# Neighbourhood attention in a two-layer hybrid block: one attention step takes a query block of one head, or of both heads of a pair side by side on the array's rows

## What is computed

```python
s_loc = jnp.einsum('bwhd,bwkhd->bhwk', qr, kw).astype(jnp.float32) + bias
s_ctx = jnp.einsum('bwhd,bshd->bhws', qr, k_ctx).astype(jnp.float32)
p = jax.nn.softmax(jnp.concatenate([s_loc, s_ctx], axis=-1), axis=-1).astype(v.dtype)
return (jnp.einsum('bhwk,bwkhd->bwhd', p[..., :n_keys], vw)
        + jnp.einsum('bhws,bshd->bwhd', p[..., n_keys:], v_ctx))
```

## Time and profile before

| | |
|---|---|
| Median of 3 runs (lowest, highest) | 2354.46 us (2350.59, 2357.75) |
| Profiled execution: its time, its span | 2355.82 us, 2354.0 us |
| TensorE busy | 2267.7 us, 96% of the span |
| VectorE, ScalarE busy | 1283.7 us (55%), 841.1 us (36%) |
| TensorE's granted clock, mean | 0.987 |
| Attention stage, layer 0 | 458.90 to 592.97 us, 134.07 us |
| Attention stage, layer 1 | 1604.68 to 1738.74 us and its last 1.5 us |

### The profile page before, as it was taken

One profiled execution on the slowest core, in us unless ns is written; L12 is line 12 of the kernel. 1 busy time (PEld: TensorE's weight loads), 2 busy tenths in 40 slices (PEclk: granted clock), 3 DMA queues, 4 the chain that ended last, 5 costly groups with the idle time before them and its releaser, 6 DMA issues.

```text
span 2354.0 us, 33977 instructions
## 1 busy us (share of the span) xinstructions
PE 2267.7 (96%) x14512; PEld 2131.6 (91%) x14512; DVE 1283.7 (55%) x1979; ACT 841.1 (36%) x1327; POOL 86.8 (4%) x160
## 2 busy tenths in 40 slices
PE   7999988999989999999979999999999999999997
PEld 3999988999978999999969999999999799999996
DVE  3555577466746867667475555225655533343434
ACT  4555332355335221221265444224543431222212
POOL 0000010000000000000000000000000000000000
PEclk9999999999999999999999999999999999999999
DMA  6212155221533543433412121232223222222121
GB/s 244 86 64 69 62 176 164 100 73 62 180 90 137 173 137 128 150 117 126 108 44 86 63 63 60 81 96 82 71 93 126 72 90 81 72 69 84 54 90 45
DMA packets 59750, 233.62 MB, mean 99 GB/s; under 512 B 7312, under 2 KB 7344, under 8 KB 57424
## 3 DMA queue, kind: packets, MB, share of 16 engines
q1 hardware_dynamic: 41040, 153.12, 20.0%
q0 software_dynamic: 18560, 78.33, 9.7%
HBM read 223.00 MB, written 8.42 MB: 98 GB/s over the span
## 4 chain that ended last, share of the span: by engine, by line
PE 86%; DVE 6%; ACT 3%; issue 2%; DMA 2%; DVEq 0%; ACTq 0%; SPq 0%; POOL 0%; POOLq 0%
PE unit L402 16%; PE unit L403 16%; PE unit L405 16%; PE unit L390 11%; PE unit L392 10%; PE unit L391 10%; DVE junk L1372 2%; PE sc L390 1%; DMA raw<-w_main 1%; PE unit L483 1%; PE sc L392 1%; PE sc L391 1%; DVE wl L1272 1%; DVE ptl L1282 1%; PE tp L654 1%
## 5 line engine op out<-in xcount | busy, mean ns | idle before, releaser
L402 PE MATMUL unit<-hmh,wh 128*128 128x320 f32 x2304 | 694.1, 309 | 1.2 <-issue 0.8
L403 PE MATMUL unit<-hml,wh 128*128 128x320 f32 x2304 | 694.0, 309 | 0.0
L1272 DVE TENSOR_TENSOR wl<-raw,wh 128x1024 fp32r<-128x1024 f32 x276 | 335.4, 1223 | 360.4 <-ACT wh L937 353.8
L405 PE MATMUL unit<-hmh,wl 128*128 128x320 f32 x2304 | 525.0, 309 | 0.0
L402 PEld LDWEIGHTS unit<-hmh,wh 128*128 128x128 f32 x2304 | 432.5, 188 | 3.3 <-issue 1.9
L403 PEld LDWEIGHTS unit<-hml,wh 128*128 128x128 f32 x2304 | 432.6, 188 | 1.5
L405 PEld LDWEIGHTS unit<-hmh,wl 128*128 128x128 f32 x2304 | 385.2, 188 | 0.0
L937 ACT ACTIVATE wh<-raw 128x1024 fp32r<-128x1024 f32 x276 | 283.8, 1049 | 120.4 <-DMA raw<-w_main 120.4
L1372 DVE CUSTOM_DVE_ANT_0 junk<-ada,csb,par 128x1024 f32<-128x1024 f32 x160 | 205.6, 1285 | 23.7 <-DMA ada<-w_ada 4.0
L390 PE MATMUL unit<-wh,hmh 128*128 128x256 f32 (+1 forms) x640 | 201.1, 314 | 12.1 <-DVE hml L1282 5.1
L392 PE MATMUL unit<-wh,hml 128*128 128x256 f32 (+1 forms) x640 | 199.3, 311 | 0.0
(11 more groups left out here) (282 smaller groups left out, 3476.0 us busy)
## 6 DMA issues: line engine op xcount, KB each, us to landing
raw<-w_main SPq DMA_DIRECT2D x276, 512.0 KB, 3.7
ada<-w_ada POOLq DMA_DIRECT2D x80, 512.0 KB, 3.9
bias<-biases POOLq DMA_DIRECT2D x16, 640.0 KB, 5.0
first<-w_first SPq DMA_DIRECT2D x8, 1024.0 KB, 21.0
x<-x POOLq DMA_DIRECT2D x2, 2560.0 KB, 12.1
gains<-g_rows POOLq DMA_DIRECT2D x4, 1024.0 KB, 5.2
x_keep<-x POOLq DMA_DIRECT2D x1, 2560.0 KB, 10.2
x<-x_keep POOLq DMA_DIRECT2D x1, 2560.0 KB, 9.6
```

The costliest lines, as they stand in the source:

```text
L402: pe.matmul(u[:, h, 0:n], a[0], xs[h][0], start=f, stop=False)
L403: pe.matmul(u[:, h, 0:n], a[0], xs[h][1], start=False, stop=False)
L405: mm = pe.matmul(u[:, h, 0:n], a[1], xs[h][0], start=False, stop=z)
L1272: dve.tensor_tensor(wl[slot[i]][:, :], raw[slot[i]][:, :], f32(wh[slot[i]][:, :]), ALU.subtract)\
```

## The change

A step is now one query block of both heads of a pair, so `STEPS` is 20 per layer. `score` issues the matmuls of the two heads in turn: head 0 on the array's rows 0 to 63 into one bank, head 1 on rows 64 to 127 into the other. `turn` transposes both heads, and the pieces come behind both, not half ahead of them. `weigh` takes each head's group one after the other, and each head has a PSUM bank of its own. The transposed weights `pth` and `ptl` of head 1 are new buffers, and they lie in slots 2 and 3 of the slabs. So slabs 46 to 55 (`NARROW` to `WIDE`) go into slots 0 and 1 alone, and `WIDE` is 56. The biases are loaded and negated in three parts. The halves of the sums are added in two parts. The splits are at steps 3, 6, 8, 11, 13, 16 and 20.

```diff
-WIDE, W_O, LAST = 58, 64, 130
+NARROW, WIDE, W_O, LAST = 46, 56, 64, 130
...
-STEPS = NPAIR * 10
+STEPS = NPAIR * 5
...
-        pth = n1("pth", [P, 2, 2, NS], F32R); ptl = n1("ptl", [P, 2, 2, NS], F32R)
+        pth = [n1("pth", [P, 2, 2, NS], F32R), at("pth1", [P, 2, 2, NS], wl_at + (RING + 2) * SLAB * 4, F32R)]
+        ptl = [n1("ptl", [P, 2, 2, NS], F32R), at("ptl1", [P, 2, 2, NS], wl_at + 2 * SLAB * 4, F32R)]
...
-            return min(32, -(-(v + 1) * 33 // 10)) if p < NPAIR - 1 else min(32, -(-(v + 1) * 8 // 3))
+            return min(32, -(-(j + 1) * 33 // 5)) if p < NPAIR - 1 else min(32, -(-(j + 1) * 32 // 7))
...
-        LIN_AT = [[3, 5, 7, 10]] * (NPAIR - 1) + [[3, 6, 9, 12]]
+        LIN_AT = [[1, 2, 3, 4]] * (NPAIR - 1) + [[1, 3, 5, 6]]
...
+        SPLIT_AT = (3, 6, 8, 11, 13, 16, 20)
...
-            may = range(RING) if j < WIDE or LAST <= j < LAST + 4 else range(RING, RING + MORE) if j >= LAST - 2 else range(RING + MORE)
+            may = range(2) if NARROW <= j < WIDE else range(RING) if j < WIDE or LAST <= j < LAST + 4 else range(RING, RING + MORE) if j >= LAST - 2 else range(RING + MORE)
...
-                    if g >= 2:
-                        pe.wait_ge(s_ready, l * STEPS + g - 1)
+                    pe.wait_ge(s_ready, (l * STEPS + i) * 2)
...
-                        product(sc[g % 2][:, 0:n], q, [t[rows, first * P:first * P + n] for t in (nkh, nkl)], True, True)
-                        mm = product(sc[g % 2][:, n:n + P], q, [t[rows, p, :] for t in (ckh, ckl)], True, True)
+                        for t, (a, b) in enumerate(terms):
+                            for hh in range(2):
+                                pe.matmul(sc[hh][:, 0:n], (nqh, nql)[a][rows[hh], j * P:(j + 1) * P],
+                                          (nkh, nkl)[b][rows[hh], first * P:first * P + n], start=t == 0, stop=t == 2)
...
-                        for head in range(2):
-                            negative_bias(head)
+                        negative_biases(0, 0)
...
-                    if g == 0:
-                        split(2)
```

More of the change, by code:

```diff
@@ L341, in build @@
         STREAMS = ((0, slice(0, NS)), (1, slice(NS, T)))
+        BIAS_AT = [slice(KIND_AT[n], KIND_AT[n] + KIND_W[n] + P) for n in range(3)]
         EARLY, CONSTS = 16 * 4, 16 * 3
@@ new lines, in score @@
+                        for t, (a, b) in enumerate(terms):
+                            for hh in range(2):
+                                mm = pe.matmul(sc[hh][:, n:n + P], (nqh, nql)[a][rows[hh], j * P:(j + 1) * P],
+                                               (ckh, ckl)[b][rows[hh], p, :], start=t == 0, stop=t == 2)
+                    else:
+                        for t, (a, b) in enumerate(terms):
+                            for hh in range(2):
+                                mm = pe.matmul(sc[hh][:, 0:P], (nqh, nql)[a][rows[hh], NS:T], (nkh, nkl)[b][rows[hh], NS:T],
+                                               start=t == 0, stop=t == 2)
@@ L644, in score @@
                     mm.then_inc(nsc_ready, 1)
[L646 to L655, removed]
@@ L657, in weigh, with turn @@
-                def weigh(head, group):
-                    pe.wait_ge(pt_ready, l * STEPS + head * 5 + (2, 4, 5)[group])
+                def turn(i):
+                    j = i % 5
+                    tiles = [BLOCKS[j][0] + n for n in range(BLOCKS[j][1])] + ["ctx"] if j < 4 else [4]
+                    for hh in range(2):
+                        g = (l * STEPS + i) * 2 + hh
+                        pe.wait_ge(d_ready, g + 1)
+                        if g >= 2:
+                            pe.wait_ge(pt_ready, g - 1)
+                        for n, t in enumerate(tiles):
+                            to = PLACE[j][t] if j < 4 else 0
+                            mm = pe.transpose(tp[hh][:, to * P:(to + 1) * P], s[:, hh, n * P:(n + 1) * P], ident[:, :])
+                        mm.then_inc(t_ready, 1)
@@ L667, in weigh @@
                     if group == 2:
[L668 removed]
+                        parts = [(vals(4), to, pch[hh][:, :], pcl[hh][:, :])]
                     else:
                         odd = (1, 0)[group]
[L671 to L674 removed]
@@ L675, in weigh @@
-                        for i in range(2):
-                            at_ = slice((i + 1) * P, (i + 2) * P)
-                            parts.append((vals(group * 2 + i), both, pth[:, group, :, at_], ptl[:, group, :, at_]))
-                    for i, (val, out, hi, lo) in enumerate(parts):
-                        pe.matmul(out, val, hi, start=i == 0, stop=False)
-                        mm = pe.matmul(out, val, lo, start=False, stop=i == len(parts) - 1)
+                        parts = [(vals("ctx"), to, pth[hh][:, group, :, 0:P], ptl[hh][:, group, :, 0:P]),
+                                 (vals(2 - group), to[:, odd * P:(odd + 1) * P], pth[hh][:, group, odd, 3 * P:], ptl[hh][:, group, odd, 3 * P:])]
@@ L681, in weigh @@
+                        for n in range(2):
+                            at_ = slice((n + 1) * P, (n + 2) * P)
+                            parts.append((vals(group * 2 + n), to, pth[hh][:, group, :, at_], ptl[hh][:, group, :, at_]))
+                    for n, (val, out, hi, lo) in enumerate(parts):
+                        pe.matmul(out, val, hi, start=n == 0, stop=False)
+                        mm = pe.matmul(out, val, lo, start=False, stop=n == len(parts) - 1)
                     mm.then_inc(pt_done, 1)
```

261 lines of the change are left out of this document (143 added, 118 removed).

## The result

The changed kernel takes **2313.9 us** (median of 4 executions, 2310.74 to 2317.51), beside 2355.57 of the kernel before in the same comparison: a ratio of 0.9819, with a 95% interval of 0.9805 to 0.9832. It is 1.8% faster. The forecast was 2340 with a range of 2331 to 2363: the sign is right, and the gain was put at a third of what it is.

A forecast was written before the change was run, and what follows sets the result against it. The prediction took TensorE's own work to bound the attention stage but for 5 us. Its terms, -15.2 - 21.8 + 24.7 + 4.4 - 6.4 = -14.3 us, gave 2341.5, or 2340 us on the median's scale, range 2331 to 2363.

The forecast's parts named there:

- 1 passages: In the attention stage, 20 visits to scores per layer instead of 40, each costing 0.38 us besides its work: -15.2 us.
- 2 two heads side by side: In the scores, the matmuls of two heads overlap, at no less than 0.063 us each: -21.8 us.
- 3 wait at the start: Ahead of each layer's first score, TensorE stands still 12.35 us for slabs 46 and 47's late transfer: +24.7 us.
- 4 low clock: Behind the new wait at the stage's start, matmuls run at a granted clock of 0.50, once per layer: +4.4 us.
- 5 waits: In the stage, waits for keys and softmax go, with 1.4 us per layer allowed for new ones: -6.4 us.
- 6 no-cost edits; outside the stages: In the stage, slightly more VectorE and ScalarE work stays hidden behind TensorE: 0 us.
- Rival C: Ahead of the first score, the wait is absent or short, with no low clock behind it: 2311 us, chance 0.05.
- floor of 0.063 us per pair of load and matmul: In the scores, least time per matmul, read from sixteen transposes; gave 14.6 us per layer for both heads' scores.
- A: In the scores, no or hardly any overlap of the two heads: 2362 us on the median's scale (+0.3%), chance 0.30.
- B: In the scores, TensorE drains at each change of row half, 0.09 us a time: 2397 us, chance 0.07.
- the 8 us of lost cover: At a pair's third step, VectorE may start late, costing up to 1 us per pair: up to +8 us.
- a price of slab 55: Slab 55's load at the end of the last piece, priced at 0, with up to 1 us per layer.

The follow-up runs named there:

- e3_twice: Changed kernel with each score's matmuls computed twice into the same banks, heads in turn both times: 2338.4 us.
- e6_piece_between: Changed kernel with a piece put between the two heads' scores, so that they can't overlap: 2352.7 us.
- e4_two_visits: Changed kernel with a piece put between near keys and context keys of each latent score, 32 more visits and no more work: 2324.0 us.
- e9_piece_then_turn: Changed kernel with one of a step's pieces put between the score and the transposes of the step before: 2315.2 us.
- e7_threes: Changed kernel with three score matmuls of head 0, then three of head 1, for near keys and then for context keys: 2312.8 us.
- e2_sequence: Changed kernel with all six score matmuls of head 0 ahead of those of head 1, instead of in turn: 2321.8 us.

## Why the prediction was wrong, point by point

Both layers together, in us, against the profiled executions. "Measured" in terms 1, 2 and 5 is worked out from the distances from start to start and from the runs above; the other lines are differences of starts and lengths.

| term | predicted | measured |
|---|---|---|
| 1 passages | -15.2 | -16.8 |
| 2 two heads side by side | -21.8 | -25.5 |
| 3 wait at the start | +24.7 | +11.7 |
| 4 low clock | +4.4 | +2.2 - 1.5 = +0.7 |
| 5 waits | -6.4 | -5.5 - 5.5 = -11.0 |
| 6 no-cost edits; outside the stages | 0 | -2.5 |
| sum | -14.3 | -43.4 (the spans: -43.3) |

**The step that failed is the wait at the start, in layer 1 (terms 3 and 4).** It had the wait in both layers, and it came in one. In layer 0 it was right: predicted 12.35 us of delay, found 11.7 and a wait of 12.0; the low clock costs the 2.2 us forecast. I had followed slots 0 to 3 through layer 0 and doubled. In layer 1 the slots stand two further, by the very reservation of the change, and slabs 46 and 47 arrive in time. That made 12.35 + 2.2 = 14.6 us too much; `e1_slots` takes 14.2 away by giving layer 0 layer 1's slots, and `e8_wait_in_both` brings the wait of 12.0 back by giving layer 1 layer 0's. Rival C priced the wait rightly: I gave it 0.05 since SyncE's and ScalarE's order spoke against it, and asked this for one layer alone. Its number, 2311, is near the 2313.9 us by chance: with its condition met in both layers `e1_slots` takes 2299.7, and the 12 us by which terms 1, 2, 5 and 6 fell short stand in for the wait of layer 0. The sentence ahead of the prediction that the same holds in layer 1 was wrong.

**Term 2 was mis-sized by 3.7 us.** The mechanism holds in full. The floor of 0.063 us per pair of load and matmul, from the earlier trace rows, made 14.6 us per layer of what takes 12.75; two heads take one head's time (0.84 beside 0.83 us; 1.01 with 384 near keys, 0.49 in the context block). The sixteen transposes load two rows each (`2*128` in the row), not a quarter of 64 or 128, and all of them the same two, so they were no measure for two halves at once. `e3_twice` and `e6_piece_between` confirm the size. Rivals A and B are out. For B: with 11 changes of row half a step in turn takes no longer than the same step with three in a row, 2312.8 beside 2313.9.

**Term 1 was nearly right.** The 0.38 us per visit holds (0.37 in `e4_two_visits`). What I left out is that a score followed by `turn` pays 0.15, not 0.19, to leave. Per layer the kernel before pays 40 x 0.38 = 15.2 us, the changed one 20 x (0.19 + 0.15) = 6.8; that is 8.4 us and not 7.6. `e9_piece_then_turn` bears the difference of the two ways out in size (0.8 us per layer). Between transposes and other matmuls on all 128 rows no time is lost. The Trainium skill's rule ("TensorEngine Tiling (Array Packing)", section Key Properties) that a change of the tiling mode drains TensorE fits the ways into and out of a score, with these 0.15 to 0.19 us.

**Term 5 was mis-sized by 4.6 us.** The waits for `nkl` and the long one for `s` went, and of the 1.4 us per layer that I allowed for the last pair 1.3 came. But I took a wait at the idle time that the profile gives, 4.8 us per layer. First, a layer before has 5.6 us of it, with two short waits beside the earlier trace rows, and a layer after has 1.5. Second, a wait costs more than the idle time. The wait of 1.6 us in the kernel before:

```profile
466.81 0.31 PE L392 MATMUL unit<-hmh,wl 128*128 128x320 f32 x1
468.73 0.66 PE L654 MATMUL tp<-ident,s 128*128 128x128 f32 x4 [1.61 <-DVE s L1611]
```

From start to start these are 1.92 us where 0.15 are usual, since the piece ran its whole 0.31 us with nothing starting beside it, and the four transposes take 0.66 us and not 0.60. So 1.83 us go with 1.61 of idle time. Over all waits of a layer the distances across a wait and behind it hold 7.6 us more than the same matmuls take elsewhere, and 2.1 in the changed kernel: 5.5 us per layer, where I had 3.2.

**Terms 4 and 6.** In layer 1 before, the wait of 1.6 us was followed by 1.5 us of low clock (the second row of the stretches of before above, 0.50), so the stages were less alike than I said. VectorE and ScalarE are busy for 80 and 72 us of the stage's 107 to 110, where I had 86 and 75, and VectorE is late only at the waits left; the 8 us of lost cover did not come, nor a price of slab 55. Of the 2.5 us outside the stages, 2.4 lie behind the last matmul (15.4 us before, 13.0 after): the last store of the output, issued at 2343.61 and now at 2302.70 us, takes 10.4 us to the end of the span before and 8.0 after. All eleven kernels of the experiments have the 8.0 too, so it comes with the changed kernel and is not scatter, but the cause stays open.

The Trainium skill's figure for four row tiles at 512 columns ("TensorE: Matmul & The Clock Gate", section Measured speedup vs the span model), by whose efficiency of 0.77 the term would be about -18 us, was further off here than full overlap: with that efficiency the doubled scores of `e3_twice` would cost 51 / (2 x 0.77), about 33 us, an estimate from that page's figure, and they cost 24.5. What the Trainium skill ("TensorEngine Tiling (Array Packing)", section PSUM Bottleneck) warns of, that tiling doesn't speed up the emptying of PSUM, did not come up: VectorE, with 80 us of work in a stage, stays under TensorE.

## What to carry over

When a ring of buffers is changed for one stage, follow the slots through every pass of the loop: an exception in the first pass shifts the second, and the same stage may stall in one and not in the other. Doubling a price that was read in one layer needs a look at the other. When the order of short visits to different kinds of work changes, count every boundary between kinds, before and after, with a distance read for each pair of kinds. Read it over two distances, since a first matmul can start early and have its time behind it, and check it against whole visits from start to start. Take a wait's price from start to start too, and not from its idle time.

## What the runs showed of the hardware

Matmuls with 64 rows on the two halves of the array overlap in full at 128, 256 and 384 columns: 0.49, 0.84 and 1.01 us for both heads, one head's time. They need not be issued in turn: each half starts its matmuls in its own order, so that a later instruction of one half was seen to start 0.12 us ahead of an earlier one of the other. Six and six cost 0.35 to 0.46 us a step, three and three nothing. Why six is too many was not tested further; that only two pairs of load and matmul can wait at a half, as the expectation of `e7_threes` has it, is a guess which the trace of `e2_sequence` allows and no run shows. Entering and leaving the 64-row form costs 0.37 us per visit, and 0.04 less where transposes follow. Transposes among other matmuls on 128 rows cost 0.11 us each and nothing for the change. A wait of 1.61 us cost 1.83. After a wait of 12.0 us the clock was at 0.50 for 4.9 us more, and 2.2 us were lost, and in layer 1 of the kernel before it fell to 0.50 after one of only 1.6 us. The same wait in layer 0 left it at 1.00.
